# One channel block of a depthwise convolution on ScalarE and GpSimd instead of VectorE

## The reference

```
proj = h @ w_in                     # -> glu a 512 | glu gate 512 | q_a 384 | kv_a 256 | k_rope 32
u    = a * sigmoid(gate)            # 512 channels
y    = depthwise_conv(u, w_dw, width 31, padding 15) + b_dw
conv = silu(layer_norm(y))          # mean and variance over the 512 channels
q    = rms_norm(rms_norm(q_a) @ w_qb);  c_kv = rms_norm(kv_a);  k, v = f(c_kv, k_rope)
out  = concat(conv, attention(q, k, v)) @ w_o
```

## Time and profile before

| | |
|---|---|
| runs | 1257.63, 1265.83, 1271.24 us (median 1265.83) |
| profiled execution | span 1265.6 us from the first to the last instruction; no other time of it is given |
| TensorE busy | 1152.1 us, 91% of the span |
| VectorE busy | 554.5 us, 44% |
| ScalarE busy | 322.6 us, 25% |
| GpSimd busy | 161.1 us, 13% |
| taps of the convolution (L1269) | 120 instructions, 66.3 us on VectorE |

### The profile page before, as it was taken

The page is one execution under the profiler, slowest core; times in us unless marked ns, Lnnn a source line. Parts: engine busy times, 40 slices in busy tenths (PEclk is TensorE's granted clock), DMA queues, the critical chain, the costliest instruction groups (busy, mean ns, idle before and its releaser), DMA issues.

```text
span 1265.6 us, 17322 instructions
## 1 busy us (share of the span) xinstructions
PE 1152.1 (91%) x6180; PEld 731.0 (58%) x6180; DVE 554.5 (44%) x1348; ACT 322.6 (25%) x773; POOL 161.1 (13%) x195
## 2 busy tenths in 40 slices
PE   4899988999749999999987999998975999999997
PEld 2456746565546555555546888776563555555554
DVE  2069566421242445444552033486134244544444
ACT  3211233432222222222132011375022222122212
POOL 4100022000121111101101041300012111111100
PEclk9699997989869999999998999999976999999999
DMA  9869822583237999999955323200205999999992
GB/s 254 301 233 337 296 100 113 202 302 115 67 151 309 405 374 367 368 378 371 363 187 178 100 100 117 84 2 2 99 34 200 374 389 366 372 368 378 354 351 84
DMA packets 76711, 301.95 MB, mean 239 GB/s; under 512 B 5540, under 2 KB 34448, under 8 KB 52080
## 3 DMA queue, kind: packets, MB, share of 16 engines
q1 hardware_dynamic: 73392, 291.03, 61.7%
q0 software_dynamic: 2832, 8.61, 2.2%
q10 hardware_dynamic: 432, 1.57, 0.3%
HBM read 291.87 MB, written 9.32 MB: 238 GB/s over the span
## 4 chain that ended last, share of the span: by engine, by line
PE 83%; DMA 4%; DVE 4%; ACT 2%; POOL 2%; issue 2%; SPq 1%; POOLq 0%; ACTq 0%; DVEq 0%; PEldq 0%
PE banks L573 31%; PE banks L815 17%; PE banks L853 14%; PE banks L837 9%; PE banks L582 4%; PE banks L611 3%; DMA a<-in_ada_w_dram 2%; PE banks L826 2%; PE banks L620 2%; DMA a<-sorted_rows 1%; PE banks L628 1%; POOL sorted_rows L1768 1%; ACT hT L982 1%; DVE a L1237 1%; DMA sorted_rows<-a,idx_sorted 1%
## 5 line engine op out<-in xcount | busy, mean ns | idle before, releaser
L815 PE MATMUL banks<-ring,a 128*64 128x256 f32 x1984 | 224.9, 379 | 3.5 <-POOL a L1780 3.5
L815 PEld LDWEIGHTS banks<-ring,a 128*64 128x64 f32 x1984 | 144.8, 137 | 99.3 <-issue 39.1
L1300 DVE SCALAR_TENSOR_TENSOR xT<-banks,mod,xT 128x128 f32<-128x128 f32 (+1 forms) x512 | 172.4, 410 | 39.8 <-PE banks L853 38.9
L853 PE MATMUL banks<-a 128*128 128x384 f32 x512 | 182.3, 499 | 3.0 <-ACT a L1030 2.6
L573 PE MATMUL banks<-ring,hT 128*128 128x256 f32 (+1 forms) x720 | 155.2, 378 | 5.8 <-ACT hT L982 5.8
L573 PEld LDWEIGHTS banks<-ring,hT 128*128 128x128 f32 x720 | 135.4, 192 | 27.3 <-issue 8.6
L1237 DVE TENSOR_TENSOR a<-a,banks 64x256 f32<-64x256 f32 x64 | 27.1, 423 | 258.8 <-ACT a L1015 258.8
L573 PE MATMUL banks<-hT,ring 128*128 128x384 f32 x384 | 129.2, 499 | 1.4 <-ACT hT L982 1.4
L853 PEld LDWEIGHTS banks<-a 128*128 128x128 f32 x512 | 91.8, 189 | 61.1 <-ACT a L1030 4.3
L837 PE MATMUL banks<-ring,a 128*64 128x512 f32 x512 | 124.0, 605 | 1.7 <-issue 1.2
L1780 POOL COPY a<-a 128x512 f32 x62 | 62.0, 999 | 455.1 <-PE banks L815 417.3
(11 more groups left out here) (196 smaller groups left out, 1086.7 us busy)
## 6 DMA issues: line engine op xcount, KB each, us to landing
ring<-in_moe_w_gate_dram SPq DMA_DIRECT2D x64, 1024.0 KB, 6.3
ring<-in_moe_w_up_dram SPq DMA_DIRECT2D x64, 1024.0 KB, 8.6
ring<-in_moe_w_down_dram SPq DMA_DIRECT2D x64, 1024.0 KB, 6.9
ring<-in_ada_w_dram SPq DMA_DIRECT2D x44, 1024.0 KB, 7.9
ring<-in_od_w_qkv_dram SPq DMA_DIRECT2D x12, 1024.0 KB, 5.1
ring<-in_ev_w_in_dram SPq DMA_DIRECT2D x6, 1024.0 KB, 12.4
a<-sorted_rows SPq DMA_DIRECT2D x12, 512.0 KB, 6.6
a<-in_ada_w_dram SPq DMA_DIRECT2D x4, 1024.0 KB, 29.6
```

Source lines behind the costliest of these rows:

```text
L815: mm = pe.matmul(bank[1][ROWS * k:ROWS * k + ROWS, 0:FF], teT[n % BUFFERS][:, c, :], w[k][:, c, :], start=(c == 0), stop=(c == KD - 1), ti ...
L853: mm = pe.matmul(bank[4 + 2 * (r % 2) + i][:, 0:TOK], y_pair[q % BUFFERS][:, P * (2 * r + i):P * (2 * r + i + 1)], weights_at[q % BUFFERS] ...
L1300: ins = ve.scalar_tensor_tensor(out=xT[:, c, a:b], in0=bank[pair + k][:, a:b], scalar=mcol(l, 5, c, j), in1=xT[:, c, a:b], op0=ALU.mult, o ...
```

## The change

The fourth channel block (block 3) leaves VectorE. `conv_taps` goes through the pairs (0, 1) and (2,); the numbers of steps stay as they were, so a step of the second round now has one instruction and not two. GpSimd, right after it has modulated the input of layer 0, makes the first tap of block 3 with bias, and then for each of the 30 other taps waits for a product, adds it to `conv_acc[:, 3, :]`, and waits for its own add. ScalarE makes the products, `uT[:, 3, k:k+399]` times the column of weights, into three buffers that lie in `pbuf`: ten after rest 0, ten after rest 1, ten after rest 2, each time behind everything else that it does for that block. Product k waits until product k-3 has been added. VectorE waits for the 30 adds before it raises `conv_ready`.

```diff
+CONV_PRODUCTS = {4: range(1, 11), 5: range(11, 21), 6: range(21, TAPS)}
...
+        products = [pbuf.rearrange("p a b -> p (a b)")[:, 512 * i:512 * i + CONVO] for i in range(3)]
...
                         if i in ADA_AFTER_BLOCK:
                             ada_copy(*ADA_AFTER_BLOCK[i])
+                        for k in CONV_PRODUCTS.get(i, ()):
+                            if k == 1:
+                                act.wait_ge(sem("u_ready"), 2 * NCH)
+                            if k > 3:
+                                act.wait_ge(sem("product_added"), k - 3)
+                            act.activation(products[k % 3], uT[:, 3, k:k + CONVO], ACT.Copy,
+                                           scale=col(C_CW + NCH * k + 3)).then_inc(sem("product_ready"), 1)
                     act.wait_ge(sem("scalar_step"), step[0])
                     act.activation(small[:, 7, 0:2 * NT], small[:, 6, 0:2 * NT], ACT.Sqrt, bias=eps[:, 0:1]).then_inc(sem("latent_std"), 1)
...
-                for pair in ((0, 1), (2, 3)):
+                for pair in ((0, 1), (2,)):
...
                         ve.wait_ge(sem("vector_step"), step[0])
+                        ve.wait_ge(sem("product_added"), TAPS - 1)
                         ve.nop().then_inc(sem("conv_ready"), 1)
...
                 modulated(l, 0)
                 if l == 0:
+                    pool.wait_ge(sem("u_ready"), 2 * NCH)
+                    link(pool.tensor_scalar(conv_acc[:, 3, :], uT[:, 3, 0:CONVO], col(C_CW + 3), col(C_CB + 3), ALU.mult, ALU.add))
+                    for k in range(1, TAPS):
+                        pool.wait_ge(sem("product_ready"), k)
+                        pool.tensor_tensor(out=conv_acc[:, 3, :], in0=conv_acc[:, 3, :], in1=products[k % 3], op=ALU.add).then_inc(sem("product_added"), 1)
+                        pool.wait_ge(sem("product_added"), k)
                     pool.wait_ge(sem("rope_loaded"), 32)
```

## The result

The changed kernel takes 1275.93 us (median of ten runs, 1273.23 to 1279.86) against 1266.34 us before (ten runs): ratio 1.0085, 95% interval 1.0066 to 1.0103, that is 10.8 us slower (8.4 to 13.0; the two medians lie 9.6 us apart). In a later session the ratio was 1.0087 (1.0057 to 1.0118). Forecast was +12.6 us, 1278.4 us, within 1268 to 1288. The profiled execution took 1279.86 us, with a span of 1278.1 us.

A forecast was written before the change was run, and what follows sets the result against it. TensorE, busy 91% of the span, was taken to wait on ScalarE's root; +12.4 (root) + 0.7 (scaling) - 0.5 (attention) + 0 (clock) = +12.6 us, giving 1278.4 us, range 1268 to 1288.

The forecast's parts named there:

- ScalarE sets the wait: End of input projection: TensorE's 3.1 us wait hangs on ScalarE's root, which the change makes 12.4 us later.
- Prices from neighbouring rows: New instructions priced from similar profiled ones: product 0.63 us, 0.52 start to start; add 1.03, 1.11 start to start.
- GpSimd's pace through three buffers: From product 11 on, three full buffers hold ScalarE to GpSimd's 1.11 us per add, delaying evictions, squares and root.
- The first batch is hidden: Ten products after rest 0: adds end by 141.4, hidden by the modulation copy of 141.45, about 1 us to spare.
- the price of a meeting: GpSimd add beside a VectorE tap: 0.68 us more per add, some three meetings, then two more, in the first batch.
- The meeting at the scaling: VectorE's scaling of q_a after the root meets add 30: 0.7 us, ends 0 and 1.1.
- The attention's relief: Attention's first six steps lose six taps: gain 0.5 us of TensorE idle time, ends 0 and 3.3.
- The clock: TensorE's granted clock after the longer wait: no difference, 3 us either way.
- equal length of all the later stages: Sign of being right: after the late root and TensorE's wait near 16 us, all stages keep their length.
- the second: Rival: GpSimd keeps up, adds at or below 0.52 us, ScalarE alone sets the pace; +5.2 - 0.5, 1270.5 us; chance 0.08.
- the first: Rival: all ten adds of the first batch pay 0.68 us, add 11 starts 2.2 us later; 1280.6 us; chance 0.15.
- the third: Rival: a later stage, waiting for something unmoved such as a weight load, absorbs the delay; 1265.8 or 1262.5 us; chance 0.07.

The follow-up runs named there:

- holding the root alone: Kernel before, nothing moved, plus 24 unread copies of 399 columns on ScalarE ahead of the root: +11.5 us (8.1 to 15.0).
- the early versions: Changed kernel, products one block earlier (12, 12, 6 after block 3, rests 0, 1); against before: three buffers -3.4, again -2.9 us; eight -1.8; no attention tap -1.9.
- the unread products: Kernel before, all taps on VectorE, plus the 30 products on ScalarE in the change's places, read by nobody: +5.7 us (2.9 to 8.6).
- the eight buffers: Changed kernel with eight product buffers instead of three, a product waiting for the add eight before it: +6.0 us against before (3.3 to 8.5).
- the kernel with the products alone: Changed kernel with GpSimd's adds left out, each product waiting only for the product three before it: trace only, TensorE's wait 8.3 us.
- the kernel of the adds alone: Changed kernel without products, GpSimd adding unscaled u 30 times from the first product's place on: +2.3 us against before (0.1 to 4.3).

## Why the prediction was right

The mechanism, step by step, is the one forecast, and the sum of 12.6 us lies in the measured 8.4 to 13.0, near its upper end.

- **ScalarE sets the wait, the root is what moves.** Shown: holding the root alone costs 11.5 us, and the early versions, with the root in its place, cost nothing. Of the root's delay 12.4 us were forecast, 12.3 measured.
- **Prices from neighbouring rows.** An add was put at 1.03 us and 1.11 from start to start; the stretch of twenty gives 1.10. A product was put at 0.63 and 0.52 from start to start; it takes 0.63, and ten unheld take 5.28.
- **GpSimd's pace through three buffers.** Shown by the unread products (5.2 us late) and by the eight buffers (6.8 us).
- **The first batch is hidden.** Right, with more room than forecast: it ends 12.9 us behind the mark and not 15.8. The step that was mis-sized is the price of a meeting: I put 0.68 us on the add, from the one pair of rows where GpSimd had waited. Here three adds met a tap in the first ten, as many as I had put there, and took 1.24 us and not 1.03: 0.2 us each. VectorE's taps paid more: ten took 8.66 us, 12.52 where adds lay beside all of them, and 6.67 in the kernel with the products alone.
- **The meeting at the scaling** was put at 0.7 us and is 0.47. The Trainium skill, "SBUF — State Buffer", section Who interferes with whom, has whoever starts first hold the shared ports for a whole instruction; the kernel of the adds alone agrees in kind, its three scalings taking 2.70 us and not 1.08. That the adds, back to back, mostly came first would explain why VectorE lost; no run separates this.
- **The attention's relief**: 0.5 us of idle time, gone as forecast.
- **The clock** was put at no difference, 3 us either way. After the profiled execution I thought that the longer wait gives 2 us back, since the stretch from TensorE's resumption to the attention took 50.5 us and not 52.5. That fell: the same stretch took 50.1 us in two of the early versions, with a wait of 3.1 us, and 52.4 in the changed kernel's second trace. Its length goes with the granted clock, a mean of 0.86 to 0.87 in the short ones and 0.81 in the long ones, and not with the wait before it. I had named equal length of all the later stages as a sign of being right; they differed by up to 2 us.

Between 12.3 + 0.5 - 0.5 = 12.3 us from the trace and the 10.8 measured lie 1.5 us, less than the interval can tell; nothing here settles them.

Of the rivals the second has its price confirmed, 5.2 us at the root, for a kernel in which GpSimd is out of the way; the first failed at the 0.68, since an add beside a tap lost 0.2; the third failed since nothing later absorbed the delay: at the first residual 10.0 us were still there.

## What to carry to other kernels

Before moving work to an idle engine, look at what that engine does next on the path: ScalarE was busy 25% of the span and still set the one wait of this stage, and ten of the thirty products stood in front of it. A producer with few buffers runs at its consumer's pace, and so does everything queued behind it; place such work where its whole stretch, at the slower engine's pace, ends ahead of the next instruction that somebody waits for. And look first for idle time of the same engine: moving twelve taps of VectorE out of the attention into its own idle time ahead of the root gave as much, within the intervals, as moving a whole block to two other engines.

## What the runs showed of the hardware

VectorE and GpSimd slow each other, and who pays depends on the pair. Beside the scalings, GpSimd's back-to-back adds kept to 0.97 to 1.17 us from start to start, while VectorE's instructions grew: scalings of q_a from 0.36 us each to 0.9, copies of 128x256 from 0.22 to 0.64. Beside taps both grew: in the early version the taps went from 0.67 to 1.25 us from start to start, and the adds beside them took 1.24 us and not 1.03 and started 1.32 apart. That is less than the 0.64 and 1.03 us of a tap and an add alone, one behind the other, so neither waited for the whole of the other. In the earlier trace rows, where VectorE's instruction began first, it was GpSimd that waited. A price for such a meeting has to be taken from the pair of instructions at hand, on both engines.

The same kernel's stages scatter by microseconds from one execution to the next, and TensorE's granted clock goes with it: the attention of layer 0 took 75.6 to 85.6 us in these traces from its first product to the turning of its outputs, 75.6 us at a mean granted clock of 0.91 and 85.6 at 0.80, and 77.2 (0.88) and 75.6 in two traces of the changed kernel. Length times clock is 68 to 69 us in all of them. The times of the kernel before show the same for the whole program, 0.9 us for 0.001 of mean clock. A gain of 3 us can't be read from two traces; it needs the rounds, and a look at the granted clock beside them.
